# A decoder trunk on one core: query, u and v tiles loaded two at a time

## The reference

```
q = (xb @ w_query).reshape(-1, 8, 2, 128)
s = einsum('thpd,pkd->thpk', q, sub_keys)        # two times 128 key scores per head
sv, si = top_k(s, 16)                            # 16 of each, their 256 sums, 16 best of these
u = u_tab[eidx];  act = gelu(einsum('thkd,td->thk', u, xb))
out = einsum('thk,thkd->td', softmax(top_s) * act, v_tab[eidx])
```

## Time and profile before

| | |
|---|---|
| median of three runs | 1613.38 us |
| profiled execution | 1615.82 us, span 1613.8 us |
| TensorE busy | 1582.1 us (98%) |
| VectorE busy | 1101.5 us (68%) |
| GpSimd busy | 494.1 us (31%) |
| DMA packets | 149979, 534.94 MB, mean 331 GB/s |
| q1, tiles and other loads issued by SyncE | 89938 packets, 314.90 MB |
| q0, gathers issued by GpSimd | 59904 packets, 218.13 MB |

### The profile page before, as it was taken

How to read it: one execution, slowest core, us unless ns; L and a number is a source line. 1 busy time by engine, 2 the same in 40 slices (tenths; PEclk the granted TensorE clock), 3 DMA queues, 4 the chain that set the end, 5 groups by cost and what they waited for, 6 DMA issues and landing times.

```text
span 1613.8 us, 30119 instructions
## 1 busy us (share of the span) xinstructions
PE 1582.1 (98%) x12128; PEld 1506.9 (93%) x12128; DVE 1101.5 (68%) x2478; ACT 209.5 (13%) x604; POOL 494.1 (31%) x423
## 2 busy tenths in 40 slices
PE   9999999999899999999999999999999999999997
PEld 7688899999899999998898888999999999999997
DVE  3373379998899998545537425999879989944441
ACT  2251221111011000000003312111211100000000
POOL 0000033335444456533300001333534435533310
PEclk9999999999999999999999999999999999999999
DMA  6304489999999999999984446999999999999991
GB/s 245 131 16 147 137 304 389 384 394 406 409 408 409 401 409 408 409 409 409 409 326 155 144 149 227 339 397 386 396 409 408 408 405 408 408 410 408 409 378 60
DMA packets 149979, 534.94 MB, mean 331 GB/s; under 512 B 17617, under 2 KB 20434, under 8 KB 149842
## 3 DMA queue, kind: packets, MB, share of 16 engines
q1 hardware_dynamic: 89938, 314.90, 50.7%
q0 software_dynamic: 59904, 218.13, 34.5%
HBM read 531.92 MB, written 1.05 MB: 330 GB/s over the span
## 4 chain that ended last, share of the span: by engine, by line
PE 79%; DVE 10%; DMA 8%; issue 3%; ACT 0%; DVEq 0%; SPq 0%; ACTq 0%; POOLq 0%
PE ps L267 37%; PE ps L1159 30%; DMA raw<-in_v_rows 6%; PE ps L1122 4%; DVE big L1322 3%; PE ps L728 2%; PE ps L279 2%; DMA big<-in_u_rows,big 2%; DVE big L1272 1%; PE ps L1501 1%; PE ps L738 1%; DVE big L1268 1%; PE ps L1433 1%; DVE big L1298 1%; DVE big L1300 1%
## 5 line engine op out<-in xcount | busy, mean ns | idle before, releaser
L267 PE MATMUL ps<-big,raw 128*128 128x160 f32 (+2 forms) x5104 | 798.5, 318 | 2.5 <-ACT big L1225 2.5
L267 PEld LDWEIGHTS ps<-big,raw 128*128 128x128 f32 x5104 | 751.5, 191 | 35.6 <-issue 3.1
L1159 PE MATMUL ps<-big,raw 128*128 128x160 f32 x4096 | 579.1, 301 | 6.5 <-DVE big L1154 2.3
L1159 PEld LDWEIGHTS ps<-big,raw 128*128 128x128 f32 x4096 | 559.6, 190 | 15.7 <-DMA raw<-in_v_rows 12.7
L1185 POOL DMA_INDIRECT big<-in_u_rows,big x208 | 250.3, 1203 | 733.4 <-DVE big L1308 376.5
L1339 DVE SCALAR_TENSOR_TENSOR big<-big 128x1024 f32<-128x1024 f32 x201 | 258.0, 1284 | 191.3 <-PE ps L1159 107.7
L1185 POOL DMA_INDIRECT big<-in_v_rows,big x208 | 240.5, 1156 | 320.6 <-DVE big L1339 255.1
L1322 DVE CUSTOM_DVE_ANT_0 big<-big 128x1024 f32<-128x1024 f32 x208 | 244.4, 1222 | 22.4 <-DMA big<-in_u_rows,big 19.8
L1225 ACT ACTIVATE big<-ps 128x160 f32<-128x160 f32 x256 | 77.4, 303 | 512.7 <-PE ps L267 474.0
L374 ACT ACTIVATE big<-h 128x272 f32<-128x272 f32 (+1 forms) x32 | 12.7, 419 | 645.8 <-DVE h L1414 597.3
L1268 DVE MAX8 big<-big 128x8 f32<-128x128 f32 (+1 forms) x99 | 33.5, 339 | 88.3 <-ACT big L1194 76.3
(11 more groups left out here) (173 smaller groups left out, 762.7 us busy)
## 6 DMA issues: line engine op xcount, KB each, us to landing
raw<-in_u SPq DMA_DIRECT2D x256, 512.0 KB
raw<-in_v_rows SPq DMA_DIRECT2D x256, 512.0 KB
raw<-in_query SPq DMA_DIRECT2D x32, 512.0 KB
raw<-in_lru_w SPq DMA_DIRECT2D x24, 512.0 KB
raw<-in_mla_down SPq DMA_DIRECT2D x17, 512.0 KB
raw<-in_mla_out SPq DMA_DIRECT2D x8, 512.0 KB
big<-in_u_rows,big POOLq DMA_INDIRECT x208
big<-in_v_rows,big POOLq DMA_INDIRECT x208
```

The lines of the kernel that those rows point to most:

```text
L267: mm = pe.matmul(out, w[:, c * P:(c + 1) * P], x[:, c, :], start=(c == 0), stop=(c == DC - 1))
L1159: return pe.matmul(accumulator(c), w, act_w[:, i, :], start=start, stop=False, skip_group_check=True)
```

## The change

The query, u and v tiles are loaded in pairs. The host lays two tiles next to each other for each partition (`by_two`), so that a DMA moves 1 MB, with 8 KB in a row in memory and, as the two slots are neighbours, in SBUF. For this the slot of tile g is (g + 1) mod 10 instead of g mod 10, as pairs begin at odd tile numbers. A pair is issued when both of its slots are free, and raises the `landed` semaphore of its first slot alone, for which both tiles' matmuls wait. MLA and LRU tiles stay single. The ring keeps ten slots. The gathers still read `u_rows` and `v_rows`, which are as before; the dense v tiles are now read from a copy laid out by two. Nothing changes in what the engines compute or in their order.

```diff
-    def __init__(self, ctx, mem, tiles):
-        self.mem, self.tiles = mem, tiles
+    def __init__(self, ctx, mem, transfers):
+        self.mem, self.transfers = mem, transfers
         self.landed = [ctx.sem(f"landed{k}") for k in range(SLOTS)]
         self.done = ctx.sem("tiles_done")
+        self.sem_of, self.count, self.total, used = [], [], 0, [0] * SLOTS
+        for count, _ in transfers:
+            k = self.slot(self.total)
+            assert k + count <= SLOTS
+            used[k] = used[k] + 16
+            self.sem_of = self.sem_of + [self.landed[k]] * count
+            self.count = self.count + [used[k]] * count
+            self.total = self.total + count
+
+    def slot(self, g):
+        return (g + 1) % SLOTS
+
+    def wait_landed(self, pe, g):
+        pe.wait_ge(self.sem_of[g], self.count[g])

     def fetch(self, sp, first, last):
-        for g in range(first, min(last, len(self.tiles))):
-            if g >= SLOTS:
-                sp.wait_ge(self.done, 2 * (g - SLOTS + 1))
-            sp.dma_start(self.mem.raw[:, g % SLOTS, :], self.tiles[g]).then_inc(self.landed[g % SLOTS], 16)
+        g = 0
+        for count, tiles in self.transfers:
+            if first <= g < last:
+                k = self.slot(g)
+                if g + count > SLOTS:
+                    sp.wait_ge(self.done, 2 * (g + count - SLOTS))
+                sp.dma_start(self.mem.raw[:, k:k + count, :], tiles).then_inc(self.landed[k], 16)
+            g = g + count
...
     def layer(n):
-        v_tiles = d[f"v_rows{n}"].rearrange("(i p) f -> i p f", p=P)
-        return ([d["query"][n][k] for k in range(2 * PH)] + [d["u"][n][k] for k in range(NK)]
-                + [v_tiles[k] for k in range(NK)])
+        return ([(2, d["query"][n][k]) for k in range(PH)] + [(2, d["u"][n][k]) for k in range(NK // 2)]
+                + [(2, d["v"][n][k]) for k in range(NK // 2)])
...
+    def by_two(tiles):
+        tiles = tiles.reshape(layers, -1, 2, P, D).transpose(0, 1, 3, 2, 4)
+        return np.ascontiguousarray(tiles)
...
-        "query": column_tiles(a["peer_w_query"]),
+        "query": by_two(column_tiles(a["peer_w_query"])),
...
-        "u": np.ascontiguousarray(u).reshape(layers, NK, P, D),
+        "u": by_two(u),
+        "v": by_two(a["peer_v"]),
```

More of the change, by code:

```diff
@@ L252, in wait_landed @@
     def wait_landed(self, pe, n):
-        g = self.base + n
-        pe.wait_ge(self.mem.tiles.landed[g % SLOTS], 16 * (g // SLOTS + 1))
+        self.mem.tiles.wait_landed(pe, self.base + n)
     def tile(self, n):
-        return self.mem.raw[:, (self.base + n) % SLOTS, :]
+        return self.mem.raw[:, self.mem.tiles.slot(self.base + n), :]
     def multiply_raw(self, pe, n, out, x, scaled=None):
@@ L1555, in layer, with single @@
     def layer(n):
-        v_tiles = d[f"v_rows{n}"].rearrange("(i p) f -> i p f", p=P)
-        return ([d["query"][n][k] for k in range(2 * PH)] + [d["u"][n][k] for k in range(NK)]
-                + [v_tiles[k] for k in range(NK)])
-    mixed = [[d["mla_down"][k] for k in range(MLA_TILES - DC)] + [d["mla_out"][k] for k in range(DC)],
-             [d["lru_w"][k] for k in range(LRU_TILES)]]
+        return ([(2, d["query"][n][k]) for k in range(PH)] + [(2, d["u"][n][k]) for k in range(NK // 2)]
+                + [(2, d["v"][n][k]) for k in range(NK // 2)])
+    def single(tile):
+        return 1, tile.unsqueeze(1)
+    mixed = [[single(d["mla_down"][k]) for k in range(MLA_TILES - DC)] + [single(d["mla_out"][k]) for k in range(DC)],
+             [single(d["lru_w"][k]) for k in range(LRU_TILES)]]
     return mixed[0] + layer(0) + mixed[1] + layer(1)
@@ L1655, in lay_out @@
     lru_in = a["lru_w_in"][0]
-    u = a["peer_u"].reshape(layers, NK, NK, DC, P).transpose(0, 1, 4, 3, 2)
+    u = a["peer_u"].reshape(layers, NK, NK, DC, P).transpose(0, 1, 4, 3, 2).reshape(layers, NK, P, D)
+    def by_two(tiles):
+        tiles = tiles.reshape(layers, -1, 2, P, D).transpose(0, 1, 3, 2, 4)
+        return np.ascontiguousarray(tiles)
     return {
```

## The result

The changed kernel takes 1633.49 us (median of 4 runs, 1630.87 to 1634.35), the kernel before, run between them, 1614.31 us (4 runs, 1613.03 to 1615.55). The ratio is 1.0116, with a 95% interval of 1.0099 to 1.0134: 19 us slower, where 6.7 were forecast, and 1.5 us above the upper end of the range. The profiled execution took 1634.35 us around a span of 1632.3, 18.5 more than before. All lines of the code in `peer` and behind have moved down by 13: the row's add L1339 is now L1352, the fold L1501 is L1514, the v tiles' matmul L1159 is L1172.

What follows compares the result with a forecast made beforehand. TensorE carries 79% of the chain, but layer 0 ends by DMA work as much as by TensorE. Layer 0 +5.2 and layer 1 +1.5 make +6.7 us on 1615.8, 1622.5; the median being 2.4 lower, forecast 1620, range 1604 to 1632.

Steps and rivals of the forecast that it cites:

- Packets: Tile and row queues both full: 8 KB served whole, turns by packet, tiles up to 273 GB/s, wanting 241.
- Cost of a packet: Tile loads: 8 KB cost 317 ns in one packet, 327 in two, 3% less; tile DMA time 1.282 to 1.243 us.
- the 415 that I had named as a limit: Layer 0, between 640 and 800 us: total GB/s rising over 415 would show the forecast wrong.
- The rows' interval: Layer 0, between 640 and 800 us: a row block every 3.0 us instead of 2.56.
- Start of layer 0's products: Layer 0: TensorE starts products 3 to 7 us late, taken as 4, after late early rows; no separate term of the sum.
- The count up to the last row: Layer 0, v tiles: last row lands at 831, last fold starts at about 832.8, 2 us later.
- The 7 us: Layer 0, 370 to 822 us: some 176 tiles each 0.039 us cheaper, saving 7 us before the last row.
- The 16 us: Layer 0: fuller ring, 134 tiles landed instead of about 121, puts 13 x 1.243 = 16 us more before the last row.
- The clock after the stop: Layer 0's last fold: TensorE stands still for 11 us, then a lower clock costs 3.4 us, bounds 0 and 6.8.
- Layer 1: Layer 1's first products: rows 7.0 us later against 5.5 us of slack, +1.5 us, bounds 0 and +6.
- Rows in time: Rival, chance 0.17: layer 0's v starvation goes and the last row lands before 820; -6 to -13 us, 1604 in the middle.
- Early stall not absorbed: Case within the forecast's 0.70: layer 0's two stops and lower clock add to the end, 4 to 7 us more, 1626.

Runs made afterwards that it cites:

- packets of 2 and 4 KB: Against the changed kernel: all query, u and v tiles single in 2 KB rows, 1647.72 us; and 1 MB pairs with 4 KB rows, 1620.74 us.
- few pairs: Against the changed kernel: all tiles single with 4 KB packets except layer 0's v tiles 72 to 81, five 8 KB pairs; first LRU tiles held back; 1619.96 us.
- four other kernels with these transfers: Changed kernel with v tiles single (1619.69 us), first LRU tiles held back (1623.21), or 150 (1628.13) or 185 (1626.07) matmuls before layer 0's last fold.
- stop filled whole: Changed kernel with 185 small unused matmuls on constants in TensorE's program before layer 0's last fold; 1626.07 us.
- v-only kernel: Changed kernel with only v tiles in 8 KB pairs, query and u tiles single with 4 KB rows; 1623.75 us.
- two pairs: Against the changed kernel: all tiles single with 4 KB packets except layer 0's v tiles 72 to 75, two 8 KB pairs; first LRU tiles held back; 1612.07 us.
- 4 KB pairs: Changed kernel with its 1 MB pairs kept, but the two tiles apart in memory, so rows are 4 KB; 1620.74 us over 8 runs.
- filled stop: Changed kernel with small unused matmuls before layer 0's last fold: 150 of them 1628.13 us, 185 of them 1626.07 us.

## Why the prediction was wrong

The direction and the mechanism were right, the size was not: forecast +6.7 us on the profiled execution, measured +18.5. Most of the gap is one sum, the count up to layer 0's last row; the rest is layer 1. Step by step:

**Packets: right.** 8 KB packets, turns by packet, tiles at 237 GB/s (forecast 241), rows at 177 (forecast about 170); shown by the packets of 2 and 4 KB and by the few pairs (608 and 614 packets).
**Cost of a packet: right in size.** 3% off on 57% of the traffic is 1.7%, and from 699 to 797 us the total of all queues rose from 409 to 415 GB/s, 1.5%: up to the 415 that I had named as a limit, not over it.

**The rows' interval: right.** 17.38 MB in 98 us are 33.1 rows, 2.96 us each (forecast 3.0); before it was 2.56.

**Start of layer 0's products: not decided.** The wait is 7.92 us (forecast 4 to 8), but TensorE starts them only 1.7 us later (forecast 4), and the wait at `placed` that I wanted to see there did not appear. In the four other kernels with these transfers it did, with 0.3 to 3.7 us, and the products start from 3.0 us earlier to 2.6 us later than before: the delay isn't clear of that spread.

**The count up to the last row: this step failed.** TensorE stood before the last fold at 839.48 - 19.90 = 819.6, as forecast (821), but the fold started at 839.48 and not at 832.8: +8.5 instead of +2, or 6.7 us too little. I had set "13 x 1.243 = 16 us more ahead of the last row" against "some 176 tiles are loaded between 370 and 822 us, each 0.039 us cheaper: 7 us". Neither came out. Here are the totals from 370 us to the landing of the last row, before (to 823) and after (to 837):

```profile
DMA packets 50660, 184.88 MB, mean 408 GB/s; under 512 B 5633, under 2 KB 5633, under 8 KB 50619
```

```profile
DMA packets 39173, 189.86 MB, mean 407 GB/s; under 512 B 4364, under 2 KB 4364, under 8 KB 27695
```

The 7 us are nothing: the mean rate didn't rise. That term assumes that DMA is never idle, and it was idle at times: 346 GB/s at 440 and 328 at 530 where I took 409. Between 425 and 629 us SyncE waited for free slots, up to 15.4 us at a time, and GpSimd for free buffers, up to 5.2, so at times nothing was left to fetch, and time saved on a packet there is no earlier row. From 425 to 629 us the two kernels' totals (before above, after below) are:

```profile
DMA packets 22751, 83.05 MB, mean 407 GB/s; under 512 B 2534, under 2 KB 2534, under 8 KB 22728
```

```profile
DMA packets 17101, 81.92 MB, mean 402 GB/s; under 512 B 1912, under 2 KB 1912, under 8 KB 12326
```

The cheaper packets should have moved more in that time, and 1.13 MB less were moved; the gain of the v tiles' stretch was used up by this. The 16 us are 12.2: 4.98 MB more, 9.5 tiles and not 13, at 408 GB/s.

Two smaller errors lie beside them. In the earlier trace rows 823.18 is where VectorE starts the add after a wait for DMA, so the row landed then, and not at 821.9. And the end was slower than counted. The last packets of the gathers were moved at 836.5 us; from 830 on they were alone, 1.68 MB, which at 408 GB/s is 4.1 us and took 6.5, since DMA's mean share sank towards the end, as with few pairs. VectorE took the last seven rows without a wait, 9.79 us, 1.40 each, and was done with the last 2.9 us behind its landing. So the landing is 823.1 + 12.2 for the tiles + 1.2 for the slower end, net of all savings, = 836.5, where I had 831, and the fold starts at 839.48. The sum is worked out from the totals; no kernel took the idle time away.

**The clock after the stop: right**, 4.0 us (forecast 3.4), shown by the stop filled whole. Layer 0 together: 12.5 where I forecast 5.2.

**Layer 1: the other term that was too small**, 6.0 us up to the last fold instead of 1.5 in the profiled execution. The line of 13 rows took 3.14 us for each, (1212.35 - 1171.51) / 13, against 3.0 forecast, and before (1191.25 - 1160.07) / 13 = 2.40, where I had put 2.56: 9.6 us later and not 7.0, with 5.5 us of slack. TensorE stopped for 3.8 us and started the products 3.1 us later, counted from the start of the LRU stage. And I charged no clock for it. The granted clock from 1216 to 1226 was 0.66, and the u piece of 32 instructions behind it took 6.77 us, which between products at full clock takes 4.43: 2.3 us more; the first products took 0.6 more. 3.1 + 2.3 + 0.6 = 6.0. The v-only kernel shows that this all belongs to the u tiles. It isn't the same in every execution: of the five kernels with u tiles in pairs two lost only 1.2 and 1.5 us in layer 1, with stops of 1.2 and 1.8 us and the clock at 1.00 behind them, and three lost 4.4 to 6.8, with stops of 3.8 to 4.0 us and a lower clock. The forecast of 1.5 holds for the first kind, and what it left out is the second.

**Range and rivals.** The upper bounds were +15 us for layer 0 and +6 for layer 1, and I put the end of the range at 1632 because I took the two not to come together. They did, with 12.5 and 6.0, as both come from packets of 8 KB. "Rows in time" wasn't the case with all v tiles in pairs, but with two pairs it was: the rows were in time, at a fold 3.25 us earlier. "Early stall not absorbed" named 1626 and had the wrong place: v tiles started 2.1 us late and TensorE still stood at the fold early enough.

**Open.** Runs of the 4 KB pairs spread over 8.6 us, and those of the kernel before over 2.3 beside them and 4.9 beside the last group. One profile of them (1620.14) shows a late last row, and none shows 1621 or more. The kernels with a filled stop fall into two groups some 6 us apart (1623, 1623 and 1629, 1631 with 185 matmuls); the two kinds of stop in layer 1 would give such a difference, but only one execution of each kernel has a profile.

## What to carry to other kernels

Where two queues are both full, the size of a packet is a priority: a longer run in a row takes bandwidth from the queue with shorter ones, so before lengthening it ask which of the two the end waits for, and give it only to the transfers whose lateness is real. A saving of DMA time counts only in stretches where DMA is at its limit; read the rate window by window before subtracting it, and remember that the kernel after can have idle stretches that the one before had not. A stop of an engine should be priced with the clock after it, and several bounds that share one cause should be added.

## What the runs showed of the hardware

- Two full queues of 4 KB and 8 KB packets moved 139 and 274 GB/s (few pairs, 692 to 708 us), of 4 and 4 KB 204 and 204 (before, 699 to 797), of 4 and 2 KB 261 and 139.5 (412 to 432). In the changed kernel the queue of 8 KB packets got the 237 GB/s that TensorE uses and left 177.
- 8 KB of tiles took 316 ns of a DMA engine in packets of 8 KB, 329 in packets of 4 KB and 345 in packets of 2 KB: the queue's share of 16 engines over its bytes, small semaphore packets included (57.1% of 98 us for 23.22 MB, 51.3% for 20.00 MB, 36.7% of 20 us for 2.79 MB). The prediction's line through two other sizes gives 317, 327 and 347.
- TensorE's idle time before the last fold against the time from it to the LRU stage, from the kernels above: 0 us 15.4 (before, filled whole, two pairs), 2.2 us 17.2, 3.4 us 20.0, 7.3 us 19.7, 13.4 us 19.1, 19.5 us 19.7, 19.9 us 19.4. In these runs the cost is there in full from 3.4 us on and doesn't grow with the stop.
- At the end of a burst the 16 DMA engines don't end together: from 822 us on half of their time was idle in the kernel with few pairs, while the last rows still landed at 2.5 us each.
